# Modulation matmuls in the seams, square sums on VectorE and an early turn of the first block

## The reference

```python
def first_block(x, ...):
    for l in range(2):
        h = rms_norm(x, g[0])
        mix = even_mixers(h) if l == 0 else fox_attention(h)      # "even", "fox"
        x = x + rms_norm(mix, g[1])
        h = rms_norm(x, g[2])
        x = x + rms_norm(conv_ffn(h), g[3])                       # "ffn0", "ffn1"

def adaln(cond, w_mod, b_mod):                                    # the modulation
    m = silu(cond) @ w_mod + b_mod                                # 1024 x 3072, for c and c_ctx
    return split(m, 3)                                            # shift, scale, gate

def second_block(x, c, ctx, c_ctx, ...):
    for layer in range(2):
        sh, sc, ga = adaln(c, w_mod[layer], b_mod[layer])
        h = rms_norm(x, g_pre[layer]) * (1 + sc) + sh
        y = even_mixer(h, h_ctx) if layer == 0 else odd_mixer(h, h_ctx)   # "even2", "odd2"
        x = x + ga * rms_norm(y, g_post[layer])
```

## Time and profile before

| | before |
|---|---|
| median of 3 runs | 1753.26 us (1750.53 to 1753.48) |
| the profiled execution | 1751.99 us, span 1750.3 us |
| granted PE clock, mean | 0.974 |
| PE / DVE / ACT / POOL busy | 1621.3 / 1093.4 / 827.6 / 139.4 us |
| instructions | 23355 |
| DMA | 217.69 MB, mean 124 GB/s |

### The profile page before, as it was taken

The page is one execution under the profiler, slowest core; times in us unless marked ns, Lnnn a source line. Parts: engine busy times, 40 slices in busy tenths (PEclk is TensorE's granted clock), DMA queues, the critical chain, the costliest instruction groups (busy, mean ns, idle before and its releaser), DMA issues.

```text
span 1750.3 us, 23355 instructions
## 1 busy us (share of the span) xinstructions
PE 1621.3 (93%) x9060; PEld 1347.4 (77%) x9060; DVE 1093.4 (62%) x1985; ACT 827.6 (47%) x1512; POOL 139.4 (8%) x153
## 2 busy tenths in 40 slices
PE   7977999988989999989999899999998879999998
PEld 7866888977868887867768676787777768887886
DVE  6666667775558868664475777615547655464565
ACT  5845444554656555442204454333324345455564
POOL 0100111111310203100000000000001000000000
PEclk9998999999999999999999999999999989999999
DMA  7433666644326544424401111124422213242333
GB/s 251 147 97 122 216 238 219 206 133 145 108 99 197 177 145 133 158 86 166 169 0 61 61 37 48 54 80 168 157 97 84 85 60 104 96 137 74 133 105 124
DMA packets 61885, 217.69 MB, mean 124 GB/s; under 512 B 7888, under 2 KB 8144, under 8 KB 61648
## 3 DMA queue, kind: packets, MB, share of 16 engines
q1 hardware_dynamic: 58608, 212.40, 36.2%
q10 hardware_dynamic: 3168, 3.80, 0.7%
...
## 4 chain that ended last, share of the span: by engine, by line
PE 64%; DVE 15%; ACT 12%; issue 6%; POOL 1%; ACTq 1%; DMA 1%; DVEq 0%; POOLq 0%
PE PS L328 18%; PE PS L330 17%; PE PS L329 17%; DVE WL L304 4%; ACT WH L293 3%; PE PS L470 2%; PE PS L2494 2%; PE PS L1936 2%; PE PS L1945 2%; PE PS L746 1%; POOL AR L1488 1%; ACT TMP L396 1%; PE PS L2525 1%; DVE AR L1437 1%; DVE X L443 1%
## 5 line engine op out<-in xcount | busy, mean ns | idle before, releaser
L304 DVE TENSOR_TENSOR WL<-RAWB,WH 128x1024 fp32r<-128x1024 f32 x346 | 429.1, 1247 | 240.0 <-ACT WH L293 236.5
L328 PE MATMUL PS<-RH,WH 128*128 128x256 f32 (+1 forms) x1560 | 504.2, 323 | 25.3 <-DVE WL L304 9.9
L329 PE MATMUL PS<-RH,WH 128*128 128x256 f32 (+1 forms) x1560 | 491.4, 315 | 0.0
L330 PE MATMUL PS<-RH,WL 128*128 128x256 f32 (+1 forms) x1560 | 491.4, 315 | 0.0
L293 ACT CAST WH<-RAWB 128x1024 fp32r<-128x1024 f32 x346 | 357.2, 1041 | 240.1 <-PE PS L330 191.7
L328 PEld LDWEIGHTS PS<-RH,WH 128*128 128x128 f32 x1560 | 299.0, 192 | 63.6 <-issue 12.0
L328 PE MATMUL PS<-WH,RH 128*128 128x512 f32 (+1 forms) x768 | 309.5, 403 | 20.7 <-DVE WL L304 12.6
L329 PEld LDWEIGHTS PS<-RH,WH 128*128 128x128 f32 x1560 | 299.5, 192 | 18.0 <-issue 0.5
L330 PEld LDWEIGHTS PS<-RH,WL 128*128 128x128 f32 x1560 | 299.0, 192 | 18.5
L329 PE MATMUL PS<-WL,RH 128*128 128x512 f32 (+1 forms) x768 | 299.4, 390 | 0.0
L330 PE MATMUL PS<-WH,RH 128*128 128x512 f32 (+1 forms) x768 | 299.4, 390 | 0.0
...
## 6 DMA issues: line engine op xcount, KB each, us to landing
RAWB<-ws SPq DMA_DIRECT2D x394, 512.0 KB, 3.6
...
```

What stands on the lines that cost most here:

```text
L304: dve.e.tensor_tensor(k.WL[:, i % SPL, :], k.RAWB[:, i % RAW, :], k.WH[:, i % SPL, :].bitcast(F32), ALU.subtract).then_inc(*dve.done("wl", i))
L328: pe.e.matmul(o, wh, xh, start=first, stop=False)
L329: pe.e.matmul(o, wh, xl, start=False, stop=False)
L330: return pe.e.matmul(o, wl, xh, start=False, stop=last)
```

## The change

1. At the seams, for the blocks 0 and 1 and with a table `SEAM_GROUP` of four seams, the squares of X's second half are summed on DVE (`squares_dve`, new, line 405), those of the first half stay on ACT.
2. The first block's root and diagonal move ahead of the second block's last gain multiplication on DVE, and ahead of its last square on ACT. The cast of the next part's first chunk moves behind both roots on ACT.
3. PE does the four units of one modulation group (0, 2, 3, 4 for the seams into ffn0, fox, ffn1, even2) ahead of the turns; the row copy stands at the end of `seam_dve`, the small turn behind the next part's first projection.
4. ffn0's loop keeps group 1 alone (units 4 to 7, steps 1 to 4), even2's loop keeps units 20 to 31 (steps 1 to 6), and the turn of group 7 stands between x1 and cv of step 7.
5. The PSUM banks of the second block's output are released for reuse only at the end of the seam.

The stream of weights is laid out in PE's order, so the sixteen chunks move in it as well.

```diff
+def squares_dve(k, dve, s, tb):
+
+    x = k.X[:, tb, half(1)]
+    junk = k.gained.take(dve, s, "p", tb)
+    dve.wait_ge(*dve.last())
+    dve.e.tensor_tensor_reduce(junk, x, x, 1.0, 0.0, ALU.mult, ALU.add, stat(k, s, "p", tb)[1]).then_inc(
+        *dve.done(s, "p", tb, "ss", 1))
+    k.gained.free(dve, s, "p", tb)
...
+def summed(k, s, kind, tb):
+
+    return (k.DVE if s in SEAM_GROUP and kind == "p" and tb < 2 else k.ACT).at(s, kind, tb, "ss", 1)
...
+SEAM_GROUP = {"ffn0": 0, "fox": 2, "ffn1": 3, "even2": 4}
...
@@ def seam_act
         put_out(second, 0)
         if m.t:
             taken_in(first, 0)
+            root_act(k, act, m.t, "p", first)
         put_out(second, 1)
         root_act(k, act, m.s, "o", second)
         if m.t:
-            taken_in(first, 1)
-            root_act(k, act, m.t, "p", first)
-            cast_to(k, act, m.opens(k))
+            taken_in(second, 0)
+            root_act(k, act, m.t, "p", second)
...
@@ def seam_dve
         residual_dve(k, dve, m.s, first, 1)
+        if m.t:
+            squares_dve(k, dve, m.t, first)
         mean_dve(k, dve, m.s, "o", second)
+        if m.t:
+            mean_dve(k, dve, m.t, "p", first)
         gained(second, 0)
         if m.t:
-            mean_dve(k, dve, m.t, "p", first)
+            root_dve(k, dve, m.t, "p", first)
+            diagonal_dve(k, dve, m.t, first, m.diag[0])
         gained(second, 1)
         root_dve(k, dve, m.s, "o", second)
         residual_dve(k, dve, m.s, second, 0)
         residual_dve(k, dve, m.s, second, 1)
...
+        if m.t:
+            squares_dve(k, dve, m.t, second)
...
+        if m.s and m.t in SEAM_GROUP:
+            mod_row_dve(k, dve, SEAM_GROUP[m.t])
...
@@ def seam_pe
+    if m.s and m.t in SEAM_GROUP:
+        g = SEAM_GROUP[m.t]
+        for u in range(4 * g, 4 * g + 4):
+            mod_pe(k, pe, u)
     for n in range(2):
         for i in range(4):
             turn_pe(k, pe, m.t, m.q, i, n, m.diag[n], n == 0)
+    if m.s and m.t in SEAM_GROUP:
+        for h in range(2):
+            k.ps.drop(m.s, "out", 1, h)
...
@@ def ffn_mod
-    return j - 1 if l == 0 and 1 <= j <= 17 else None
+    return j + 3 if l == 0 and 1 <= j <= 5 else None
...
@@ def even2_pe
     for j in range(8):
         project(k, pe, (s, "x1", j), "e_w_in", 8 + j, rhs, 512, ready)
-        mod_unit_pe(k, pe, 16 + 2 * j, j == 0)
+        if j == 0:
+            mod_turn_pe(k, pe, SEAM_GROUP[s])
+        elif j < 7:
+            mod_unit_pe(k, pe, 18 + 2 * j, j == 1)
+        else:
+            mod_turn_pe(k, pe, 7)
         project(k, pe, (s, "cv", j), "e_w_in", 16 + j, rhs, 512, ready)
-        mod_unit_pe(k, pe, 17 + 2 * j)
-    mod_turn_pe(k, pe, 7)
+        if 0 < j < 7:
+            mod_unit_pe(k, pe, 19 + 2 * j)
```

55 lines of the change are left out of this document (32 added, 23 removed).

## The result

| | before | changed |
|---|---|---|
| median, first set of runs | 1752.85 us (4 runs, 1750.53 to 1753.48) | 1738.67 us (4 runs, 1735.93 to 1740.76) |
| ratio and 95% interval | | 0.9921 [0.9903, 0.9938] |
| profiled execution, and its span | 1751.99, 1750.3 us | 1738.86, 1737.1 us |

The change is faster by 14.2 us in this set. I had forecast 19.3, so the gain is half to three quarters of the forecast. The forecast time, 1733.0, is 5.7 us too low. The measured 1738.67 lies 1.7 us above the forecast's own range (1729 to 1737); it is inside the wide one (1726 to 1740), which had been widened for rivals that were not the main cause of the miss.

What follows compares the result with a forecast made beforehand. PE was taken to bound the kernel, full in ffn0's loop and idle at seams; 12.0 + 4.3 + 2.4 + 1.6 - 0.5 - 0.5 + 0 = 19.3 us off 1751.99 gave 1732.7, said as 1733; range 1729 to 1737, wide 1726 to 1740.

Steps and rivals of the forecast that it cites:

- Moved units: Sixteen modulation units leave full PE stretches (twelve ffn0, 0.78 us each; four even2, 0.66 each) for idle seams: -12.0 us.
- the small turns cost nothing: A group's little turn matmuls and DVE's row copy only change place between full stretches: costed at nothing.
- second hole: PE's 1.34 us wait for WL near ffn0's start, one of two expected to go with the earlier ctx load.
- Turn of group 7: In even2, a projection between copy and turn removes PE's 2.93 us wait and the transposes' half pace: -4.3 us.
- The ctx load: Near ffn0's start, ctx issued earlier removes two PE holes waiting for WL: -2.4 us, bounds 0 and -2.4.
- The seams: Norm reordering at the four seams: -1.6 us at even-ffn0, +0.5 at ffn0-fox and fox-ffn1, 0 at ffn1-even2.
- the second gap: At ffn0-fox, PE waits 3.2 to 3.4 us before the second block's turns; the clock is taken to fall.
- rival 1: The clock holds through the seams: gain 22.6 us, to 1729.4; chance 0.17.
- rival 5: At the seams the weight ring has no room, late chunks hold the turns: slower, up to 1809 us; chance 0.02.
- The square sum at full pace: DVE's new square sum at the seams, 512 wide, takes 0.70 us plus 0.08 for the accumulator read.
- rival 2: DVE's square sum streams at half pace, 1.3 us each, 3.9 us in all: 1736.6; chance 0.09.
- The 2 us of clock falls elsewhere: Allowance in the forecast's own range for clock falls elsewhere that shift when everything before them moves: 2 us.

Runs made afterwards that it cites:

- units_back: Changed kernel with the four units of group 0 put back into ffn0's steps 1 to 4: 1743.72 us, 0.9956 of before.
- even2_both: Changed kernel with group 4's small turn behind cv(0) and the mid-tile weight cast of even2 moved behind the tiles: 1732.48 us, 0.9899 of before.
- ctx_early: Kernel before with only the load of the ctx rows sent at chunk 36 instead of 40: 1749.78 us, 0.9997 of before.
- turn7_only: Kernel before with only unit 31 moved ahead of cv(7) and group 7's turn behind it: 1752.94 us, 1.0017 of before.
- turn7_ahead: turn7_only with both casting engines looking one chunk further ahead at x1(7): 1747.98 us, 0.9984 of before.
- the second execution: Changed kernel unaltered, run again in the second set as the measure for others: 1740.7 us, 0.9938 of before.
- the third: Changed kernel unaltered, run once more in the third set: 1737.89 us, 0.9924 of before.
- old_norm: Changed kernel with the seams' norm put back as before (all square sums on ACT, old order): 1739.67 us, 0.9939 of before.
- norm_only: Kernel before with only the new norm order at the seams; units, turns and ctx load unmoved: 1749.32 us, 0.9995 of before.
- turn4_late: Changed kernel with even2's small turn of group 4 behind cv(0) on PE and DVE: 1734.11 us, 0.9912 of before.
- cast_late: Changed kernel with the cast and weight load in the middle of even2's normed tiles moved behind them: 1737.35 us, 0.9923 of before.
- best2: even2_both with the norm of before at all four seams: 1735.82 us, 0.9917 of before.

## Why the prediction was right, and where it wasn't

**Moved units: right.** 0.78 us in ffn0 was measured by units_back (0.8), 0.66 in even2 fits what the first two projections gain in even2_both (1.10, where two units less and a small turn more make 0.95). That the small turns cost nothing was off: one costs 0.46 us in ffn0. Two of the four of ffn0 leave it, which makes ffn0's gain 12 x 0.78 + 2 x 0.46 = 10.3, and with the second hole's 1.25 it is 11.5 of the 11.64 measured. The two that left stand in fox and ffn1 now. In ffn1 the next matmul starts 0.36 us behind the turn's start; in fox 1.02, of which PE waits 0.52 for DVE's use of the result (line 812), the same hand-over as in even2 on a smaller scale. So this error nearly cancels but for what follows.

**Turn of group 7: right, with luck in the size**, 4.3 forecast and 4.6 measured. The 2.9 us of waiting are gone, as forecast. The other 1.6 of the term, the transposes at half pace, I had tied to that wait, and ctx_early has the wait without it: that part is there or not by the execution. A projection between the copy and the turn is not enough alone: turn7_only and turn7_ahead have it too, and they lose by the look-ahead of the casts and by the turn's result being read directly behind it.

**The ctx load: mis-sized.** The step was "The two holes go: **-2.4 us**". One, of 1.25 us, waits for a chunk that lands late, and ctx is at most a part of why; the other stands behind a table load in ACT's queue and is still there in the changed kernel (1.09 us). The bound of 0 that the prediction gave this term was left out of its own range. I had read the wait's releaser (WL, from DVE) and the longest landing in the chain, and had not looked at what ACT did before its cast. And executions of before's order without the second hole are common (two traces of four): the term is 0 to 1.25 us.

**The seams: right in their bounds, by a mechanism that hangs on the clock.** Forecast +0.5, +0.5 and 0 for the three later ones, measured -0.17, -0.24, -0.44, in the second execution +1.09, +0.05 and +0.08, in the third 0.00, -0.72 and -0.02 (from the same starts). The prediction's step was that the clock falls behind the second gap, and that this makes a loss of a gain. At the seam fox-ffn1 the traces with units and new norm show it: -0.71 to -0.73 in the four where the clock doesn't fall, -0.23 and +0.04 in the two with 3.4 us of half clock, +0.84 in the one with 6.8. So rival 1 (the clock holds) comes true at single seams in some executions. What was off is how long the half clock lasts. The medians of old_norm and norm_only say that the new order is worth nothing that can be told. The units in the seams are indeed hidden; rival 5 (the weight ring has no room) shows no trace of itself, the turns of the first block begin 0.91 us behind the units for want of the diagonal, not of a chunk.

**The square sum at full pace: right, rival 2 wrong.** Two fp32 operands in SBUF and an accumulator take 693 ns at 512 wide, less than the 748 ns of line 458 without one. By the rule of the Trainium skill that I weighed ("Vector Engine (DVE) Microarchitecture Reference", "Points that are easy to get wrong") it would have streamed at half the pace, 1.3 us with its read by the prediction's working, where the rows give 693 + 83 ns. The instruction here is named a custom one in the profile; the rule speaks of the scalar-tensor-tensor shape, and no run here shows that shape with an accumulator and two such operands.

**What I missed: even2's start.** Two steps of the prediction failed, and both put a term at nothing.

The first: the little turn matmuls and DVE's row copy "only change place; I cost them at nothing". The small turn of group 4 stands ahead of cv(0), which takes the PSUM bank that the turn has used, and its release is queued on DVE behind the convolution of x1(0). It costs 3.7 to 4.4 us with the half clock behind it, shown by turn4_late.

The second: "At ffn1-even2 the DVE paces eight normed tiles afterwards, so PE's clock matters less: 0, bounds 0.4 either way." That looked at the turns alone. In before, the chunk that stands second in even2 was a modulation unit, so the cast in the middle of the tiles was nothing (PE waits 0.43 us there, at 768.31, as ahead of the next tile); moving the unit away made it a real one. It costs 1.74 us of PE's wait, shown by cast_late.

Together they are the 6.0 to 6.8 us between the changed kernel (4.94 to 5.68 lost) and even2_both (1.10 gained); the profiled execution missed the forecast by 6.1. The 2 us of clock falls elsewhere that the range allowed for were needed as well: ffn1 lost 2.0 us in two executions and 0.3 in the third.

So the mechanism (PE time taken off full stretches and put into idle ones) is confirmed and the sum was 6 us too large. That the time still fell into the wide range is luck in part: the range had no term for either of the two waits. With the two waits mended the kernel stands at 1732.5 us.

**Open.** What the new norm order is worth: best2 against even2_both says 3.3 us, old_norm and norm_only say nothing. Summed over the four seams, the traces with units and the new norm in all of them stand at -3.9 to +0.8 us (six), those with units and the old norm at +0.1 and +2.9 (two), too few to settle it. Open too is why the second hole, and the half clock behind one and the same wait, come in some executions only.
